# Turning the late tiles through device memory instead of on TensorE, in a hybrid encoder layer on one core

## The chip, the cores and the metric

One core of a Trainium2 chip runs the whole program. The metric is the time of one execution on the device in microseconds (us). The kernel before has a median of 942.22 us over 3 runs (942.02 to 943.11).

## The reference

One encoder layer over 256 tokens with 2048 channels, all in float32. The input is normalised and modulated by vectors made from `c` (`w_ada`), multiplied by one wide matrix `w_in`, and its columns feed three branches:

```
mod = silu(c) @ w_ada + b_ada;  shift, scale, gate = split(mod, 3)
h = rms_norm(x, norm_g) * (1 + scale) + shift
proj = h @ w_in      # pool_u, pool_z, q, k, v, attn_z, conv_a, conv_b, conv_z, gates
y_pool = multiscale_pool(pool_u, pool_w, pool_scale) * silu(pool_z)
y_attn = window_attention(q, k, v, attn_sink) * silu(attn_z)
y_conv = conformer_conv(conv_a, conv_b, ...) * silu(conv_z)     # ends in @ conv_pw (1024 x 1024)
g_pool, g_attn, g_conv = split(sigmoid(gates), 3)
merged = g_pool * (y_pool @ w_branch_pool) + g_attn * (y_attn @ w_branch_attn) + g_conv * (y_conv @ w_branch_conv)
x = x + gate * (merged @ w_out)
out = rms_norm(x, final_g)
```

`shift`, `scale` and `gate` are vectors of 2048, one value for each channel. All matrices together are more than 150 MB, and each is read once.

## The kernel before

**Pieces.** All large products are cut into 152 pieces, numbered m = 0 to 151. A piece is 512 rows (four tiles of 128) by 512 columns of a weight matrix, 1 MB. A chunk is the set of pieces that add up into one block of 256 tokens x 512 columns; it fills one of two accumulators in PSUM, `acc_even` or `acc_odd`, which the chunks take in turn. Each float32 operand is split into a high half (`wh`, `act_h`) and a low half (`wl`, `act_l`), and a product takes three matmuls (lines 1246, 1247, 1248). With four tiles and two halves of the tokens a piece is 24 matmuls of 512 columns.

**The weights' way.** SyncE issues the load of a piece into one of four `raw` buffers. ScalarE rounds it to `wh` (L466) once the piece four places earlier has been used, VectorE subtracts to get `wl` (L759), and then the `raw` buffer is free for the next load. In the loop over m ScalarE and VectorE both end step m with their share of piece m + 4. Every engine works its list in order, so a wait in step m holds back all that stands behind it.

**The order of the late pieces.** 88 to 91 `zc1`; 92 to 95 the attention branch `ba0`, `ba1`; 96 to 103 the gates `ga2`, `ga3`; 104 to 107 `ba2`, `ba3`; 108 to 111 `pw0`, `pw1` (the pointwise product of the convolution); 112 to 119 `gc0`, `gc1`; 120 to 123 `bc0`, `bc1`; 124 to 131 `gc2`, `gc3`; 132 to 135 `bc2`, `bc3`; 136 to 151 the four result chunks `o0` to `o3`, four pieces each (K tiles 0 to 3, 4 to 7, 8 to 11, 12 to 15).

**LayerNorm of the convolution**, steps 92 to 101: VectorE sums (L1151, L1160), TensorE adds over partitions after pieces 93 and 97 (L1459), VectorE scales (L1168), ScalarE applies SiLU (L700) and takes the high half (L706), VectorE the low half (L1172).

**Transposes.** `zs_conv` (the gated convolution output, two blocks) and `merged` (the merged branches, four blocks of 512 channels) are in token layout and are needed with channels on partitions. For each of these six late blocks TensorE runs eight 128x128 transposes (`transpose4`, L1291) into a side bank, `side_a` or `side_b`; ScalarE copies the high half out (L474), VectorE the low half (L775). A semaphore `y_ready` counts the blocks that are done: `bc0` waits for 5 and 6, piece i of `o0` for 7 + i.

**Gate vector.** `gate` is made from 16 loads of 1 MB of `w_ada`, put between the loads of the pieces (GATE_AFTER). For each, VectorE runs four multiply-adds into `gate_sums` (L1083 and L1089, `gate_piece`), in the step that splits the piece of that number. After four loads ScalarE takes the high half (L717), VectorE the low half (L1187), TensorE sums over partitions with a matrix of ones (L1560, L1561, 512 columns each), and VectorE adds the row to `gate_rows` (L1194). Quarter q + 1 starts only when quarter q's matmuls are done.

**The end.** `o0` to `o2` are multiplied by the gate and added to the residual by VectorE (`residual`, L1098 and L1102), which frees the accumulator; ScalarE squares and sums them (L613), VectorE scales them by `final_g` (L1110). For `o3` the gate is multiplied into the four weight pieces instead (`gate_weights`, L771): VectorE does that for piece m + 2 right behind the split of m, for m from 146 on, and ScalarE's split of pieces 148 to 151 waits for it. The last four pieces run by half of the tokens.

**GpSimd** only issues the small loads. Late in the kernel these are `x_res` (2 MB, L439), `final_rows` (L440) and `gate_rows` (L442).

Of the kernel before, what the change touches and what calls it, by code (L numbers as in the profile page):

```python
# [4 lines left out]
P = 128  # L5
D_MODEL, SEQ = 2048, 256
TH = SEQ // P
# [60 lines left out]
GATE_AFTER = (112, 113, 115, 116, 118, 119, 121, 122, 124, 125, 127, 128, 130, 131, 133, 134)  # L68
# [44 lines left out]
QUAD = 32  # L113


def program(nc, a, out):
# [71 lines left out]
    zs_conv = [at("zs_conv0", [P, TH, COLS], F32, 192 * KB), at("zs_conv1", [P, TH, COLS], F32, 196 * KB)]  # L188

# [40 lines left out]
    with ctx:  # L230
# [60 lines left out]
        merged_ready = sem("merged_ready")  # L291
        gate_summed, gate_rows_mm, gate_added = sem("gate_summed"), sem("gate_rows_mm"), sem("gate_added")
# [68 lines left out]
        def score_step(u):  # L361
            return 71 + 2 * u

# [40 lines left out]
        def _(pool):  # L404
# [10 lines left out]
            for row, name, rows in ((V_NORM_G, "norm_g", 16), (V_B_ADA, "b_ada", 32),  # L415
# [22 lines left out]
            pool.wait_ge(used, END["pw1"])  # L438
            pool.dma_start(x_res[:, :, :], x_rows).then_inc(x_res_loaded, 16)  # L439
            pool.dma_start(final_rows[:, :], a["final_g"].partition_broadcast(P)).then_inc(final_loaded, 16)  # L440
            pool.wait_ge(y_t, 4)
            pool.dma_start(gate_rows[:, :], a["b_ada"][0, 2 * D_MODEL:3 * D_MODEL].partition_broadcast(P)  # L442
                           ).then_inc(gate_b_loaded, 16)

        @block.scalar
        def _(act):
# [28 lines left out]

            def by_tiles(bank_):
                return bank_[:, :].rearrange("p (t s) -> p t s", t=4)
# [138 lines left out]
            for m in range(OPENING - WIDTH - RING + 1, M_END):  # L616
# [90 lines left out]
                if m in (111, 113):  # L707
                    b = (m - 111) // 2
                    spread(y_h[:, 4 * b:4 * b + 4, :], by_tiles((pa, pb)[b]), y_t, 3 + b, y_high)
                if m in (113, 119, 125, 131):  # L710
                    q = (m - 113) // 6
# [7 lines left out]
                if m in (131, 133, 135, 137):  # L719
                    j = (m - 131) // 2  # L720
                    spread(act_h[:, 4 * j:4 * j + 4, :], by_tiles((pb, pb, pa, pb)[j]), y_t, 5 + j, y_high)
                if m in (140, 144, 148):
                    for h in range(TH):
                        square_result((m - 140) // 4, h, (m - 140) // 4 + 1)
# [880 lines left out]
```

## Time and profile before

| | value |
|---|---|
| median of 3 runs | 942.22 us |
| the profiled execution, its own time | 942.33 us |
| its span | 940.5 us |
| TensorE matmul busy | 911.0 us (97%), 4211 matmuls |
| VectorE busy | 703.0 us (75%) |
| ScalarE busy | 420.6 us (45%) |
| GpSimd busy | 9.2 us (1%) |
| loads on the SyncE queue | 67.1% of the 16 DMA engines' span |
| read from memory | 217.24 MB |

The time has 1.8 us outside the span. The span is cut below by stretch. "PE" is TensorE's matmuls, "DVE" VectorE, "ACT" ScalarE, "POOL" GpSimd, and a trailing q means the queue of the engine. In a row of the timeline the first number is the start from the span's beginning, the second how long the row covers, and what stands in brackets is how long the engine was idle before it and which engine ended that. A matmul's 0.39 us is its own length; they overlap, so the step from one start to the next is what counts.

### The profile page before, as it was taken

The numbers are of one execution on the slowest core, as the hardware profiler recorded it, in microseconds if no ns is written. First come the engines' busy times: TensorE is split into PE (matmuls) and PEld (weight loads), VectorE is DVE, ScalarE is ACT, GpSimd is POOL, SyncE is SP. The second block draws the span as 40 slices with busy tenths as digits, with TensorE's granted clock in tenths as the row PEclk, the third lists the DMA queues.
The fourth block names the chain that finished last, engine by engine and source line by source line (L and its number), as shares of the span: only waits on it lengthen the run. The fifth ranks groups of instructions, "written<-read, shape, count | busy, mean of one in ns | idle before, by whom it ended". The sixth has DMA issues, their size and how long they took to land.

```text
span 940.5 us, 10296 instructions
## 1 busy us (share of the span) xinstructions
PE 911.0 (97%) x4211; PEld 732.9 (78%) x4211; DVE 703.0 (75%) x794; ACT 420.6 (45%) x388; POOL 9.2 (1%) x26
## 2 busy tenths in 40 slices
PE   1999999999999999999999999999999999999996
PEld 1667777888888888888877777888888888888885
DVE  4778787878968777767688786685687988865783
ACT  3445252645344334444375655347433443444332
POOL 2000000000000000000000000000000000000000
PEclk9999999999999999999999999999999999999999
DMA  9999999855446556555545456656879998955512
GB/s 337 387 386 386 385 332 388 311 179 179 160 155 213 189 182 208 193 179 179 183 138 171 139 159 149 208 171 153 271 241 394 374 335 276 352 207 191 182 45 90
DMA packets 108208, 220.01 MB, mean 234 GB/s; under 512 B 3858, under 2 KB 3938, under 8 KB 107393
## 3 DMA queue, kind: packets, MB, share of 16 engines
q1 hardware_dynamic: 106768, 213.15, 67.1%
q0 software_dynamic: 1104, 5.42, 1.5%
q8 instruction: 33, 0.54, 0.2%
q10 hardware_dynamic: 288, 0.79, 0.2%
q14 instruction: 15, 0.11, 0.0%
HBM read 217.24 MB, written 2.10 MB: 233 GB/s over the span
## 4 chain that ended last, share of the span: by engine, by line
PE 90%; DVE 4%; DMA 3%; ACT 2%; issue 1%; SPq 0%; DVEq 0%; ACTq 0%
PE acc_odd L1246 13%; PE acc_odd L1248 13%; PE acc_odd L1247 13%; PE acc_even L1246 12%; PE acc_even L1248 12%; PE acc_even L1247 12%; PE side_a L1246 2%; PE side_a L1248 2%; PE side_a L1247 2%; PE side_b L1306 2%; DMA raw<-in_w_ada 1%; DVE gate_sums L1089 1%; DMA x_tok<-in_x 1%; PE side_b L1246 1%; PE side_a L1291 1%
## 5 line engine op out<-in xcount | busy, mean ns | idle before, releaser
L759 DVE TENSOR_TENSOR wl<-raw,wh 128x2048 fp32r<-128x2048 f32 x147 | 336.0, 2290 | 147.8 <-ACT wh L466 147.5
L466 ACT ACTIVATE wh<-raw 128x2048 fp32r<-128x2048 f32 x147 | 280.2, 1913 | 261.3 <-PE acc_odd L1248 105.7
L1246 PE MATMUL acc_odd<-wh,act_h 128*128 128x512 f32 x432 | 169.8, 393 | 0.0
L1246 PE MATMUL acc_even<-wh,act_h 128*128 128x512 f32 x430 | 169.7, 395 | 0.0
L1247 PE MATMUL acc_odd<-wl,act_h 128*128 128x512 f32 x432 | 168.2, 389 | 0.0
L1248 PE MATMUL acc_odd<-wh,act_l 128*128 128x512 f32 x432 | 168.2, 389 | 0.0
L1248 PE MATMUL acc_even<-wh,act_l 128*128 128x512 f32 x430 | 167.6, 390 | 0.0
L1247 PE MATMUL acc_even<-wl,act_h 128*128 128x512 f32 x430 | 167.4, 389 | 0.0
L974 DVE SCALAR_TENSOR_TENSOR conv_slots<-conv_slots,taps 128x256 f32<-128x256 f32 x240 | 100.2, 479 | 0.2
L1246 PEld LDWEIGHTS acc_even<-wh,act_h 128*128 128x128 f32 x430 | 80.7, 188 | 19.5 <-issue 2.8
L1246 PEld LDWEIGHTS acc_odd<-wh,act_h 128*128 128x128 f32 x432 | 81.1, 188 | 18.9 <-issue 2.2
L1248 PEld LDWEIGHTS acc_odd<-wh,act_l 128*128 128x128 f32 x432 | 81.1, 188 | 17.1
L1248 PEld LDWEIGHTS acc_even<-wh,act_l 128*128 128x128 f32 x430 | 80.7, 188 | 17.1
L1247 PEld LDWEIGHTS acc_odd<-wl,act_h 128*128 128x128 f32 x432 | 81.1, 188 | 16.4
L1247 PEld LDWEIGHTS acc_even<-wl,act_h 128*128 128x128 f32 x430 | 80.8, 188 | 16.1
L805 DVE SCALAR_TENSOR_TENSOR ada_sums<-raw,small,ada_sums 128x512 f32<-128x512 f32 x60 | 45.1, 752 | 7.8 <-DMA raw<-in_w_ada 5.9
L1089 DVE SCALAR_TENSOR_TENSOR gate_sums<-raw,small,gate_sums 128x512 f32<-128x512 f32 x60 | 45.0, 751 | 1.7
L1246 PE MATMUL acc_odd<-wh,y_h 128*128 128x512 f32 x96 | 37.6, 392 | 0.0
L1246 PE MATMUL acc_even<-wh,y_h 128*128 128x512 f32 x96 | 37.5, 390 | 0.0
L1248 PE MATMUL acc_even<-wh,y_l 128*128 128x512 f32 x96 | 37.4, 389 | 0.0
L1248 PE MATMUL acc_odd<-wh,y_l 128*128 128x512 f32 x96 | 37.4, 389 | 0.0
L1247 PE MATMUL acc_odd<-wl,y_h 128*128 128x512 f32 x96 | 37.4, 389 | 0.0
(294 smaller groups left out, 925.8 us busy)
## 6 DMA issues: line engine op xcount, KB each, us to landing
raw<-in_w_in SPq DMA_DIRECT2D x106, 1024.0 KB, 5.1
raw<-in_w_ada SPq DMA_DIRECT2D x48, 1024.0 KB, 9.3
raw<-in_w_out SPq DMA_DIRECT2D x16, 1024.0 KB, 5.0
raw<-in_w_branch_pool SPq DMA_DIRECT2D x8, 1024.0 KB, 5.0
raw<-in_w_branch_attn SPq DMA_DIRECT2D x16, 512.0 KB, 6.7
raw<-in_w_branch_conv SPq DMA_DIRECT2D x8, 1024.0 KB, 6.4
raw<-in_conv_pw SPq DMA_DIRECT2D x4, 1024.0 KB, 5.9
x_tok<-in_x SPq DMA_DIRECT2D x2, 1024.0 KB, 9.2
```

Of the source, the lines that this page charges most:

```text
L466: nc.scalar.activation(wh[:, m % RING], raw[SLOT_OF[g]][:, :, :], ACT.Copy).then_inc(high_done, 1)
L759: nc.vector.tensor_tensor(wl[:, m % RING], raw[SLOT_OF[load_of(m)]][:, :, :], wh[:, m % RING].bitcast(F32), ALU.subtract).then_inc(raw_don ...
L805: last = nc.vector.scalar_tensor_tensor(ada_sums[:, :], src, column, ada_sums[:, :], ALU.mult, ALU.add)
L974: ins = nc.vector.scalar_tensor_tensor(sums, window, tap, sums, ALU.mult, ALU.add)
L1089: last = nc.vector.scalar_tensor_tensor(gate_sums[:, :], src, column, gate_sums[:, :], ALU.mult, ALU.add)
L1246: nc.tensor.matmul(sums, xh, wh[:, slot, i, :], start=begin, stop=False)
L1247: nc.tensor.matmul(sums, xh, wl[:, slot, i, :], start=False, stop=False)
L1248: return nc.tensor.matmul(sums, xl, wh[:, slot, i, :], start=False, stop=end)
L1291: ins = nc.tensor.transpose(dst[:, SEQ * t + P * h:SEQ * t + P * (h + 1)], src(h, t), ident[:, :])
L1306: ins = nc.tensor.matmul(pb[rows, 0:COLS], c_wide[:, PK * i + t, :], raw[SLOT_OF[g]][:, t, :], start=(i == 0), stop=(i == 3), tile_positio ...
```

## The change

The six late blocks are no longer transposed on TensorE. VectorE transposes 32x32 squares (two instructions of 128x512 a block, `turn_blocks`) into a buffer `blocks`; GpSimd stores that to a scratch array in device memory with four DMAs of 32 partitions each (`store_blocks`), waits until all have landed, and loads it back in the other layout (one DMA for each block of `zs_conv`, two for each of `merged`). ScalarE and VectorE then take the halves from SBUF instead of PSUM. The two `blocks` buffers alternate, and the last two blocks also wait until the block two before them is back.

The 16 gate loads start after piece 98 instead of 112; the steps of the gate's halves and sums move to 101, 110, 120, 130 (ScalarE and VectorE) and 102, 111, 121, 131 (TensorE). The four gate rows each get a half of a side bank of their own, and are added into `gate_rows` at 123, 124, 128 and 134.

`o0` and `o1` alternate: pieces 136 to 143 are `o0` 0, `o1` 0, `o0` 1, `o1` 1 and so on, so each K block of `merged` is first needed two pieces later than the last. `residual` for `o0` moves from step 140 to 143, and the first two `scale_result` from 142 and 146 to 145 and 146. GpSimd's `gate_rows`, `x_res` and `final_rows` loads come later.

```diff
+TURNING = ("o0", "o1")
+START = sum(_pieces for _, _pieces in CHUNKS) - 4 * PK
...
+        if _name in TURNING:
+            _at = START + 2 * _i + TURNING.index(_name)
...
-GATE_AFTER = (112, 113, 115, 116, 118, 119, 121, 122, 124, 125, 127, 128, 130, 131, 133, 134)
+GATE_AFTER = (98, 100, 102, 104, 107, 109, 111, 113, 116, 118, 121, 123, 126, 128, 131, 133)
...
+    blocks = [at(f"blocks{s}", [P, 4, 4, TH, QUAD], F32, (176 + 4 * s) * KB) for s in range(2)]
+    scratch = [nc.dram_tensor(f"turned_{g}", (QUAD, 4, 4 * TH, 4, QUAD), F32, kind="Internal").ap() for g in range(TURNS)]
...
+            def store_blocks(g):
+
+                pool.wait_ge(blocks_ready, g + 1)
+                for a_ in range(4):
+                    pool.dma_start(scratch[g].rearrange("j b n a i -> j (b n) a i")[:, :, a_, :],
+                                   blocks[g % 2][QUAD * a_:QUAD * (a_ + 1), :, :, :, :].rearrange("j b t h i -> j (b t h) i")
+                                   ).then_inc(blocks_stored, 16)
+                pool.wait_ge(blocks_stored, 16 * 4 * (g + 1))
+
+            def load_merged(g):
+                rows = scratch[g].rearrange("j b (q n) a i -> q b j (n a i)", q=2)
+                for q in range(2):
+                    pool.dma_start(by_channels(g)[:, q, :, :].rearrange("p t s -> p (t s)"), rows[q]
+                                   ).then_inc(turned[g], 16)
+
+            for b in range(2):
+                store_blocks(b)
+                pool.dma_start(zs_conv[b][:, :, :].rearrange("p h c -> p (h c)"),
+                               scratch[b].rearrange("j b n a i -> b j (n a i)")).then_inc(turned[b], 16)
+            pool.wait_ge(y_ready, 6)
...
+            for g in range(2, TURNS):
+                store_blocks(g)
+                load_merged(g)
...
-                if m in (113, 119, 125, 131):
-                    q = (m - 113) // 6
+                if m in (118, 119):
+                    b = m - 118
+                    spread(y_h[:, 4 * b:4 * b + 4, :], turned_tiles(b), turned[b], 16, y_high)
+                if m in (101, 110, 120, 130):
+                    q = (101, 110, 120, 130).index(m)
                     act.wait_ge(raw_done, raws(LOAD_OF["gate", q, 3]))
...
+                if m in (132, 133, 138, 140):
+                    j = (132, 133, 138, 140).index(m)
+                    act.wait_ge(used, END["gc3"])
+                    spread(high_tiles(j), turned_tiles(2 + j), turned[2 + j], 16 * 2, y_high)
...
+            def turn_blocks(g, src):
+
+                for h in range(TH):
+                    last = nc.vector.transpose(blocks[g % 2][:, :, :, h, :].rearrange("p b t i -> p t b i"),
+                                               src[:, h, :].rearrange("p (t b j) -> p t b j", t=4, b=4))
+                last.then_inc(blocks_ready, 1)
...
+                if m == 112:
+                    for b in range(2):
+                        dve.wait_ge(*freed(f"pw{b}"))
+                        turn_blocks(b, zs_conv[b][:, :, :])
...
+                if m in (122, 124, 134, 136):
+                    j = (122, 124, 134, 136).index(m)
+                    dve.wait_ge(merged_ready, 9 + j)
+                    if j > 1:
+                        dve.wait_ge(turned[j], 16 * 2)
+                    turn_blocks(2 + j, merged[:, :, bass.ts(j, COLS)])
+                if m in (101, 110, 120, 130):
+                    dve.wait_ge(sums_high, (101, 110, 120, 130).index(m) + 1)
                     nc.vector.tensor_tensor(gate_low[:, :], gate_sums[:, :], gate_high[:, :].bitcast(F32), ALU.subtract
                                             ).then_inc(sums_low, 1)
...
-                if m in (140, 144, 148):
-                    if m == 140:
+                if m in (132, 133, 138, 140):
+                    j = (132, 133, 138, 140).index(m)
+                    low_halves(7 + j, high_tiles(j), low_tiles(j), turned_tiles(2 + j))
+                if m in (143, 144, 148):
+                    if m == 143:
                         dve.wait_ge(gate_added, 4)
                         dve.wait_ge(x_res_loaded, 16)
-                    residual((m - 140) // 4)
-                if m in (142, 146, 150):
-                    scale_result((m - 142) // 4)
+                    residual((143, 144, 148).index(m))
+                if m in (145, 146, 150):
+                    scale_result((145, 146, 150).index(m))
...
-                elif name == "o0":
+                elif name in TURNING:
                     pe.wait_ge(y_ready, 7 + i)
...
-                if m in (131, 133, 135, 137):
-                    j = (m - 131) // 2
-                    pe.wait_ge(merged_ready, 9 + j)
-                    if j == 2:
-                        pe.wait_ge(gate_added, 4)
-                    else:
-                        pe.wait_ge(y_ready, (6, 7, 0, 8)[j])
-                    transpose4((pb, pb, pa, pb)[j], block_of(merged, COLS * j), y_t)
+                if m in (102, 111, 121, 131):
+                    q = (102, 111, 121, 131).index(m)
+                    pe.wait_ge(sums_low, q + 1)
+                    pe.wait_ge(var_ready, 2)
+                    pe.wait_ge(y_ready, 4)
+                    nc.tensor.matmul(gate_bank(q), ones_high[:, :], gate_high[:, :], start=True, stop=False)
+                    nc.tensor.matmul(gate_bank(q), ones_high[:, :], gate_low[:, :], start=False, stop=True
+                                     ).then_inc(gate_rows_mm, 1)
```

## Rows read from the trace of the kernel before

**Rows 1.** Windows: start:end, span, busy time and instructions of each engine, clock, DMA

```profile
600.00:640.00 40.00, 40.00 (x178) 33.09 (x177) 35.72 (x21) 17.05 (x10) 0.00 (x0) 1.00 0.59 171
700.00:770.00 70.00, 69.91 (x316) 57.57 (x315) 57.91 (x54) 28.66 (x20) 1.83 (x3) 1.00 1.01 369
840.00:870.00 30.00, 30.00 (x142) 24.96 (x142) 17.80 (x12) 12.90 (x9) 0.00 (x0) 1.00 0.59 201
```

**Rows 2.** Timeline of ScalarE, two splits in a row, one piece apart

```profile
883.38 1.92 ACT L466 ACTIVATE wh<-raw 128x2048 fp32r<-128x2048 f32 x1 [3.52 <-PE acc_odd L1248]
888.82 1.92 ACT L466 ACTIVATE wh<-raw 128x2048 fp32r<-128x2048 f32 x1 [3.52 <-PE acc_odd L1248]
```

**Rows 3.** Timeline of TensorE around a transpose of eight

```profile
706.13 0.39 PE L1248 MATMUL acc_odd<-wh,conv_low 128*128 128x512 f32 x1
706.37 1.03 PE L1291 MATMUL side_a<-ident,zs_conv 128*128 128x128 f32 x8
707.16 0.47 PE L1246 MATMUL acc_even<-wh,act_h 128*128 128x512 f32 x1
707.47 0.39 PE L1247 MATMUL acc_even<-wl,act_h 128*128 128x512 f32 x1
```

**Rows 4.** Timeline of TensorE before the first gate row

```profile
724.27 0.39 PE L1248 MATMUL acc_even<-wh,act_l 128*128 128x512 f32 x1
724.75 0.50 PE L1560 MATMUL side_a<-gate_high,ones_high 128*128 128x512 f32 x1
```

**Rows 5.** Timeline of VectorE, steps 94 to 98

```profile
616.64 2.29 DVE L759 TENSOR_TENSOR wl<-raw,wh 128x2048 fp32r<-128x2048 f32 x1
620.73 2.29 DVE L759 TENSOR_TENSOR wl<-raw,wh 128x2048 fp32r<-128x2048 f32 x1 [1.80 <-ACT wh L466]
...
625.34 3.84 DVE L1160 TENSOR_REDUCE ln_stat<-squares 128x256 f32<-128x2048 f32 x1
```

**Rows 6.** Timeline of VectorE, two gate pieces: quarter's first, and a later one

```profile
694.17 0.48 DVE L1083 TENSOR_SCALAR gate_sums<-raw,small 128x512 f32<-128x512 f32 x1
694.69 2.33 DVE L1089 SCALAR_TENSOR_TENSOR gate_sums<-raw,small,gate_sums 128x512 f32<-128x512 f32 x3
...
712.51 3.11 DVE L1089 SCALAR_TENSOR_TENSOR gate_sums<-raw,small,gate_sums 128x512 f32<-128x512 f32 x4
715.53 1.22 DVE L1180 TENSOR_TENSOR zs_conv<-acc_odd,zs_conv 128x1024 f32<-128x1024 f32 x1
```

**Rows 7.** Timeline of VectorE, steps 99 to 102

```profile
654.13 2.29 DVE L759 TENSOR_TENSOR wl<-raw,wh 128x2048 fp32r<-128x2048 f32 x1 [1.32 <-ACT wh L466]
656.34 2.28 DVE L1172 TENSOR_TENSOR conv_low<-conv_slots,c_h 128x2048 fp32r<-128x2048 f32 x1
```

**Rows 8.** Timeline of ScalarE: pieces 97 and 102 end, halves of the gate

```profile
629.66 1.92 ACT L466 ACTIVATE wh<-raw 128x2048 fp32r<-128x2048 f32 x1 [3.52 <-PE acc_even L1248]
...
657.34 1.92 ACT L466 ACTIVATE wh<-raw 128x2048 fp32r<-128x2048 f32 x1 [1.43 <-PE acc_odd L1248]
...
754.67 0.63 ACT L717 ACTIVATE gate_high<-gate_sums 128x512 fp32r<-128x512 f32 x1 [0.83 <-DVE gate_sums L1089]
```

**Rows 9.** Timeline of VectorE: low half of the gate, and the tail

```profile
724.00 0.69 DVE L1187 TENSOR_TENSOR gate_low<-gate_sums,gate_high 128x512 fp32r<-128x512 f32 x1 [0.90 <-ACT gate_high L717]
...
892.98 2.28 DVE L771 TENSOR_TENSOR raw<-raw,gate_rows 128x2048 f32<-128x2048 f32 x1
895.18 1.22 DVE L1098 TENSOR_TENSOR out_tmp<-acc_odd,gate_rows 128x1024 f32<-128x1024 f32 x1
...
911.02 4.49 DVE L759 TENSOR_TENSOR wl<-raw,wh 128x2048 fp32r<-128x2048 f32 x2
```

**Rows 10.** DMA issues: queue, number, KB, us from issue to landing

```profile
x_res<-in_x POOLq DMA_DIRECT2D x1, 2048.0 KB, 10.8
pool_w<-in_pool_w POOLq DMA_DIRECT2D x1, 1024.0 KB, 6.2
...
gate_rows<-in_b_ada POOLq DMA_DIRECT2D x1, 1024.0 KB, 7.8
...
small<-in_attn_sink POOLq DMA_DIRECT2D x1, 8.0 KB, 2.7
```

**Rows 11.** Groups of GpSimd: busy, mean ns of one issue, idle before

```profile
L433 POOL DMA_DIRECT2D pool_w<-in_pool_w x1 | 0.9, 937 | 0.0
...
L442 POOL DMA_DIRECT2D gate_rows<-in_b_ada x1 | 0.5, 541 | 11.4 <-PE side_b L1291 11.4
```

More of the change, by code:

```diff
@@ L113 @@
 QUAD = 32
+TURNS = 6
 def program(nc, a, out):
@@ L291, in program @@
         merged_ready = sem("merged_ready")
+        blocks_ready, blocks_stored = sem("blocks_ready"), sem("blocks_stored")
+        turned = [sem(f"turned_{g}") for g in range(TURNS)]
         gate_summed, gate_rows_mm, gate_added = sem("gate_summed"), sem("gate_rows_mm"), sem("gate_added")
@@ L362, in score_step, with by_tiles, gate_bank, turned_tiles @@
             return 71 + 2 * u
+        def by_tiles(bank_):
+            return bank_[:, :].rearrange("p (t s) -> p t s", t=4)
+        def gate_bank(q):
+            return (pa, pb)[q // 2][:, bass.ts(q % 2, COLS)]
+        def turned_tiles(g):
+            return by_channels(g) if g >= 2 else zs_conv[g][:, :, :].rearrange("p h (t s) -> p (h t) s", t=2)
+        def high_tiles(j):
+            return act_h[:, 4 * j:4 * j + 4, :].rearrange("p (q t) s -> p q t s", q=2)
+        def low_tiles(j):
+            return act_l[:, 4 * j:4 * j + 4, :].rearrange("p (q t) s -> p q t s", q=2)
+        def by_channels(g):
+            return merged[:, :, bass.ts(g - 2, COLS)].rearrange("p q (t s) -> p q t s", t=2)
         @block.sync
@@ L474, in spread @@
                 nc.scalar.activation(dst, src, ACT.Copy).then_inc(signal, 1)
-            def by_tiles(bank_):
-                return bank_[:, :].rearrange("p (t s) -> p t s", t=4)
             act.wait_ge(c_loaded, 16)
@@ L1193, in _ @@
                     row = gate_rows[:, bass.ts(q, COLS)]
-                    nc.vector.tensor_tensor(row, row, pa[:, 0:COLS], ALU.add).then_inc(gate_added, 1)
-                if m in (131, 133, 135, 137):
-                    j = (m - 131) // 2
-                    tiles = slice(4 * j, 4 * j + 4)
-                    low_halves(7 + j, act_h[:, tiles, :], act_l[:, tiles, :], (pb, pb, pa, pb)[j])
-                if m in (140, 144, 148):
-                    if m == 140:
+                    nc.vector.tensor_tensor(row, row, gate_bank(q), ALU.add).then_inc(gate_added, 1)
+                if m in (132, 133, 138, 140):
+                    j = (132, 133, 138, 140).index(m)
+                    low_halves(7 + j, high_tiles(j), low_tiles(j), turned_tiles(2 + j))
+                if m in (143, 144, 148):
+                    if m == 143:
                         dve.wait_ge(gate_added, 4)
                         dve.wait_ge(x_res_loaded, 16)
-                    residual((m - 140) // 4)
-                if m in (142, 146, 150):
-                    scale_result((m - 142) // 4)
+                    residual((143, 144, 148).index(m))
+                if m in (145, 146, 150):
+                    scale_result((145, 146, 150).index(m))
                 for i in range(taps_done, taps_done + TAPS_AT.get(m, 0)):
```

46 lines of the change are left out of this document (10 added, 36 removed).

## The prediction

> **What bounds the kernel now.** I read the page first: TensorE is busy for 97% of the span and nearly all of the chain that ended last is its matmuls. Then the windows of the stretch that the change touches [rows 1]: TensorE is busy for 40.00 of 40, 69.91 of 70 and 30.00 of 30 us, at full granted clock. It is the only engine without slack, and a saving counts only if it shortens TensorE's own list or a wait in it. The beat is in ScalarE's splits [rows 2]: each starts when a piece ends, and they are 5.44 us apart, so a piece is 24 matmuls at 0.227 us. VectorE is the second engine: 35.72 of 40 us busy in steps 93 to 98 and 57.91 of 70 behind piece 111, but only 17.80 of 30 in the stretch 840 to 870. The DMA engines are full in the stretch of the gate loads (1.01) and 0.59 busy in the other two. No TensorE wait comes from that, so moving the gate loads gives back nothing by itself.
>
> **Removed: six transposes.** Around one of them [rows 3] the start of the last matmul before and of the second after are 1.34 us apart; without the eight transposes these two steps are 0.46 us. So 0.88 us each, 6 x 0.88 = 5.3 us less. The three other edits to TensorE's list are neutral in work: four pairs of gate matmuls stay, and pieces 136 to 143 only change order. Before the first gate row TensorE waits: 724.27 to 724.75 is 0.48 instead of 0.23 us [rows 4]; the third row's is alike. These two waits, 0.5 us, go with the old places. Credit: 5.8 us.
>
> **Wait 1, at piece 97 (0.6 us).** Gate piece 0 now follows the split of piece 98 on VectorE. It costs 2.85 us (694.17 to 697.02) [rows 6]. VectorE was idle for 1.80 us there, until 620.73 [rows 5]; free at 618.85, it now starts that split at 621.7, 1.0 us late. The reduction that started at 625.34 and took 3.84 us ends at 630.15 instead of 629.18. TensorE's column sums stand behind piece 97, which ended at 629.57 [rows 8]: they wait 0.6 us.
>
> **Wait 2, at piece 102 (5.3 us): the dearest step.** TensorE sums the first gate row right behind piece 102, and for that waits for the low half of the sums. The last gate piece of this quarter is bound to the split of piece 104, which VectorE started at 654.13 [rows 7], held there by ScalarE's long LayerNorm step. Behind it stand now: the gate piece, 3.03 us [rows 6], the low half of the convolution, which was next at 656.34 (2.2 us) [rows 7], and the low half of the gate, 0.69 us [rows 9]; ScalarE's high half (0.63) [rows 8] fits beside the second. 656.34 + 3.03 + 2.2 + 0.69 = 662.3. Piece 102 ended at 657.26 (ScalarE's split behind it started at 657.34) [rows 8]. That is 5.0 us; the split of 104 itself slips by about 0.8 (gate pieces 0 and 1 push the scaling before SiLU by 3.7 us, of which some 3 had been slack), while piece 102 slips by the 0.6 of wait 1. I take 5.3. Behind the waiting sum stand pieces 103 and on, so TensorE gets nothing back. The second, third and fourth rows (pieces 111, 121, 131) have their last gate piece one piece earlier against the wait; by the same count they just fit, within 0.5 us.
>
> **Wait 3, at the end of `o0` (2.4 us), and 0.2 us before `o1`.** Before, `o0` ended four pieces ahead of `o2`, which needs the same accumulator. Now it ends with piece 142 and `o2` starts at 144, one piece (5.44 us) later. VectorE comes to `residual` only behind the split of 146 and the gating of 148: ScalarE 1.92 [rows 2], VectorE 2.2 and 2.2, then the multiply that frees the bank, 1.22 [rows 9], and some 0.25 of hand-overs: 7.8 us. TensorE waits 2.4. The same sum without the gating is 5.6 us for `bc3`'s bank before the first piece of `o1`: 0.2 us.
>
> **Wait 4, in the last four pieces (1.0 us).** The late `residual` pushes ScalarE's square and sum, the splits of 147 to 149, and the two `scale_result` that now stand before the splits of 149 and 150. Before, the pair of splits that ends the list ran 911.02 to 915.5 [rows 9]; the first of the pair was 2.4 us ahead of its need. Adding the steps up, the split of 150 ends some 6.1 us later, TensorE's need only 2.7 us later (the sum so far): 6.1 - 2.7 - 2.4 = 1.0 us.
>
> So without anything from the DMAs: -5.8 + 0.6 + 5.3 + 0.2 + 2.4 + 1.0 = +3.7 us. VectorE's twelve transposes lie in its slack; the nearest rows for one of 128x512 are 0.48 and 0.69 us [rows 6, 9], I take 0.62, or 1.24 us a block.
>
> **Wait 5, the way through memory.** The trace has no such store. The last two blocks decide, since `merged` block 2 is done two pieces ahead of block 3, and GpSimd's list is serial: store, wait, load, next store. Take the end of piece 135 as 0. Block 2 is ready at -2.4, block 3 at +8.0 (split of 139, merge, turn). TensorE needs block 3 at piece 142, 6 x 5.44 + 0.2 = 32.8; with the halves (ScalarE 1.0, VectorE 1.2) and hand-overs it must be back at 30.4. With S for a store and L for a load: back at -2.4 + S + 1.0 + S + L, if S is over 9.4. L: two issues of 0.5 us, then 4.5 us (rows from 2.7 us for 8 KB to 7.8 for 1 MB [rows 10]), 5.5 in all. S: four issues of 1024 runs of 128 bytes each. Floor for one: its issue, 0.94 us, as `pool_w` of 1024 runs [rows 11]. Ceiling: `pool_w` itself, eight times the bytes in as many runs, 6.2 less the 2.7 of a tiny one [rows 10], 3.5 us. I take 2.0, between, because count speaks for one end and bytes for the other. Four are 8 us alone; beside the weight loads, which hold 0.59 of the DMA engines [rows 1], about 11.5, plus 2.7 to land: S = 14.3. Back at 32.7, 2.3 us late; I take 2.5 us. At the floor (S about 7) nothing waits. At the ceiling S is 16.7 alone and over 20 beside the loads: 7 to 15 us here, and some more at `bc0` and the third gate row.
>
> The Trainium skill ("DMA: Bandwidth & Descriptors", Specifications) puts the least transfer for full rate at 512 bytes and says smaller ones make the DMA engine read, modify and write. It speaks against runs of 128 bytes, towards the ceiling; no row here shows such a store to memory.
>
> **Sum.** 3.7 + 2.5 = +6.2 us on the profiled execution's 942.33 (span 940.5 and 1.8 around it), 948.5 us. That execution is 0.1 us over the median, which I don't correct for.
>
> **Rivals.**
> 1. The memory way is hidden: S under 13. For it: 128 KB a DMA is little, and nothing else is on GpSimd's queue. 942.3 + 3.7 = 946.0. Chance 0.30.
> 2. The memory way binds outright, S 17 or more: tile 3 is late by 7 to 15 us, and blocks 0 and 1 are late for `bc0` too, since both are turned in one step at 112 and pass GpSimd one behind the other; each 2 us of S adds 4 at the end. 953 to 970, most likely 958. For it: 24,576 short runs in all. Chance 0.22.
> 3. GpSimd can't write its DMA work while VectorE runs: every issue waits for the end of a split or gate piece (2.3 to 3 us [rows 6]), 4 x 2.3 = 9 us a store, 2 x 9 - 4 late at the end: about 960. Against it: `gate_rows` was issued at 0.54 us [rows 11] in the middle of a split, and landed in 7.8 us [rows 10] with the DMAs full. The Trainium skill ("SBUF — State Buffer", SBUF: two separate sides) has this as a lock of the port that VectorE and GpSimd share. By the issue row the trace doesn't bear it out. Chance 0.04.
> 4. The other sign: wait 2 is not there. The one mechanism is the place of VectorE's last gate piece: if ScalarE handed over piece 104 at least 5 us sooner, or the row's matmuls found their input before piece 102 ends at 657.9, wait 2 is 0, and with S under 13 the sum is 3.7 - 5.3 = -1.6, 940.7 us. It decides faster from 3.5 us of the 5.3 on. Against it: rows 7 are the present order, and nothing in the change makes ScalarE's LayerNorm step earlier. Chance 0.04 for faster; 0.06 for within 0.2%, where it is only part gone.
>
> My forecast, 947 to 953 by wait 5 of 1 to 7 us, has 0.34. Slower by over 0.2% (1.9 us, about what a measurement of this kernel can tell from no change) is then 0.34 + 0.30 + 0.22 + 0.04 = 0.90. Range 944.8 to 963: rival 1 at the low end with 1 us of error in the waits, most of rivals 2 and 3 at the top; about 0.10 lies below and 0.10 above.
>
> **What would show it.** In the profile after: no L1291 rows on `merged` or `zs_conv`; the first gate row's matmul with an idle of 4.5 to 6 us before it, ended by VectorE's low half; an idle of 2 to 3 us before the first matmul of piece 144, ended by L1098's successor in the file; the fourth block's wait before piece 142, ended by the low half, itself behind a DMA. Wrong would be: a first gate row without a wait (rival 4), waits at pieces 120 or 121 (rival 2), or GpSimd issue rows of over 2 us (rival 3).

## The result, and the profile of the changed kernel

The changed kernel has a median of 953.96 us over 4 runs (953.34 to 956.9), the kernel before 942.25 us (942.02 to 943.11) in the same comparison. The ratio is 1.013, 95% interval 1.0118 to 1.0142: 12 us slower, where +6 was predicted. The sign was right. The time lies inside the stated range, but above my forecast of 947 to 953 and in the part that belongs to rival 2, and rival 2's cause was not at work: that it came to lie there is no merit of the sum.

The profiled execution of the changed kernel took 956.9 us, with a span of 955.1, 14.6 over the span before. That is 3 us more than its median and the longest of the four, so the sizes below are those of a slightly long execution.

TensorE's timeline, stretches around its longest idle times. Columns: start, duration, engine, line, operation, operands, count, and in brackets the idle time before it with what ended it.

```profile
657.43 0.39 PE L1312 MATMUL acc_odd<-wl,act_h 128*128 128x512 f32 x1
657.66 0.39 PE L1313 MATMUL acc_odd<-wh,act_l 128*128 128x512 f32 x1
663.12 0.80 PE L1615 MATMUL side_a<-gate_high,ones_high 128*128 128x512 f32 x1 [5.07 <-DVE gate_low L1253]
663.72 0.63 PE L1616 MATMUL side_a<-gate_low,ones_high 128*128 128x512 f32 x1
664.15 0.63 PE L1311 MATMUL acc_odd<-wh,act_h 128*128 128x512 f32 x1
664.57 0.63 PE L1312 MATMUL acc_odd<-wl,act_h 128*128 128x512 f32 x1
...
826.54 0.39 PE L1313 MATMUL acc_odd<-wh,act_l 128*128 128x512 f32 x1
830.93 0.80 PE L1615 MATMUL side_b<-gate_high,ones_high 128*128 128x512 f32 x1 [4.00 <-DVE gate_low L1253]
...
899.49 0.39 PE L1313 MATMUL acc_odd<-wh,act_l 128*128 128x512 f32 x1
902.16 0.50 PE L1311 MATMUL acc_even<-wh,act_h 128*128 128x512 f32 x1 [2.29 <-DVE out_tmp L1154]
...
929.27 0.39 PE L1313 MATMUL acc_odd<-wh,act_l 128*128 128x512 f32 x1
930.51 0.50 PE L1311 MATMUL acc_odd<-wh,act_h 128*128 128x512 f32 x1 [0.85 <-DVE wl L809]
```

To read a loss out of it, take the distance between two starts and subtract the usual step, 0.227 us: 663.12 - 657.66 - 0.23 = 5.2 us. A second loss has no bracket at all: behind the first gate row the matmuls start 0.42 apart instead of 0.227 (664.15 and 664.57) and last 0.63 instead of 0.39. The windows show why (columns as in [rows 1], the last three being the granted clock, the DMA share and GB/s):

```profile
663.00:669.00 6.00, 5.88 (x14) 4.63 (x15) 4.47 (x3) 1.74 (x1) 0.00 (x0) 0.50 1.05 316
669.00:680.00 11.00, 11.00 (x50) 9.12 (x49) 3.60 (x4) 6.04 (x4) 0.00 (x0) 1.00 0.45 155
...
831.00:836.50 5.50, 5.50 (x13) 4.36 (x14) 4.10 (x2) 4.61 (x4) 0.00 (x0) 0.51 0.74 255
836.50:845.00 8.50, 8.50 (x39) 7.02 (x38) 4.92 (x4) 2.86 (x2) 0.00 (x0) 1.00 0.60 226
```

TensorE ran at 1.2 GHz for 6 us behind the 5.2 us wait, and again behind the 4.2 us wait. Between 663 and 669 it is 5.88 us busy, so this loss can't be found by looking for idle time. Its size also differs from run to run. The 5.2 us wait at piece 102 stands unchanged in four of the kernels below, and the loss behind it was 1.9, 2.2, 1.6 and 1.9 us there (`e3_xres_late`, `e4_long`, `e8_res142`, `e10_by_b`) as against 2.8 here. In `e10_by_b` the granted clock was 0.50 already from 660.5 us on, with TensorE idle, and full again from 666.7; here it was still 0.90 from 660.5 to 662.7, and the low stretch fell on the matmuls.

All that TensorE lost or gained, each by the distance of starts:

| Place | us |
|---|---|
| six transposes, old gate-row waits gone | -5.8 |
| piece 97, column sums (wait 1) | +0.6 |
| first gate row, piece 102 (wait 2) | +5.2 |
| low clock behind it | +2.8 |
| third gate row, piece 121 | +1.1 |
| fourth gate row, piece 131 | +4.2 |
| low clock behind it | +2.6 |
| first piece of `o1`, first of `o2` (wait 3) | +0.25, +2.4 |
| last four pieces (wait 4) | +1.0 |
| sum; difference of the spans | +14.4; +14.6 |

The fourth gate row wasn't in my sum. Its chain in the trace, on ScalarE and then on VectorE:

```profile
816.02 1.92 ACT L517 ACTIVATE wh<-raw 128x2048 fp32r<-128x2048 f32 x1 [4.89 <-DMA raw<-in_w_branch_conv]
822.22 1.92 ACT L517 ACTIVATE wh<-raw 128x2048 fp32r<-128x2048 f32 x1 [4.28 <-DMA raw<-in_w_branch_conv]
829.52 0.63 ACT L765 ACTIVATE gate_high<-gate_sums 128x512 fp32r<-128x512 f32 x1 [5.39 <-DVE gate_sums L1145]
```

```profile
824.17 2.29 DVE L809 TENSOR_TENSOR wl<-raw,wh 128x2048 fp32r<-128x2048 f32 x1 [3.90 <-ACT wh L517]
826.38 3.11 DVE L1145 SCALAR_TENSOR_TENSOR gate_sums<-raw,small,gate_sums 128x512 f32<-128x512 f32 x4
830.18 0.69 DVE L1253 TENSOR_TENSOR gate_low<-gate_sums,gate_high 128x512 fp32r<-128x512 f32 x1 [0.70 <-ACT gate_high L765]
```

The last gate piece is bound to VectorE's split, the split to ScalarE's, and ScalarE's to a weight load that lands 4.28 us after ScalarE is free. The matmuls of the weights have pieces in hand and don't notice. The gate row has none, so it takes the whole delay. The releaser in TensorE's bracket, `gate_low`, is only the last link. The DMA issues (columns as in [rows 10]) and ScalarE's waits for loads (us in total, times, longest) belong to it:

```profile
raw<-in_w_branch_conv SPq DMA_DIRECT2D x8, 1024.0 KB, 12.4
turned<-blocks POOLq DMA_DIRECT2D x24, 128.0 KB, 5.8
...
merged<-turned POOLq DMA_DIRECT2D x8, 256.0 KB, 8.3
...
zs_conv<-turned POOLq DMA_DIRECT2D x2, 512.0 KB, 14.4
```

```profile
ACT wh L517 <- DMA raw<-in_w_branch_conv: 22.7, 5, 6.6
ACT wh L517 <- DMA raw<-in_w_in: 22.3, 7, 6.8
```

The landing times are medians, and the waits are those from 600 to 955 us. In the kernel before, the eight loads of `in_w_branch_conv` landed in 6.4 us, and in the same stretch ScalarE waited 7.2 and 3.4 us for these two. GpSimd's timeline of the last two blocks shows how long the way through memory took:

```profile
853.68 3.10 POOL L472 DMA_DIRECT2D turned<-blocks  x4 [42.52 <-DVE blocks L830]
862.31 1.38 POOL L480 DMA_DIRECT2D merged<-turned  x2 [5.53 <-DMA turned<-blocks]
864.70 3.10 POOL L472 DMA_DIRECT2D turned<-blocks  x4 [1.00 <-DVE blocks L830]
876.34 1.38 POOL L480 DMA_DIRECT2D merged<-turned  x2 [8.54 <-DMA turned<-blocks]
```

A store of four is 862.31 - 853.68 = 8.6 us and 11.6 us here, not 14.3, and TensorE doesn't wait for block 3. The stores of the first four blocks took 6.4, 17.3, 11.5 and 12.4 us, also without a TensorE wait of their own.

### The profile page after: what moved, and what is told of

It reads as the page before. It is cut to its first block, busy times and chain, and to the rows that moved or that the text cites. A ratio compares the mean times of both kernels' runs of the same rounds, so it can differ in the third digit from the quotient of the medians.

```text
span 955.1 us, 10249 instructions
## 1 busy us (share of the span) xinstructions
PE 912.0 (95%) x4163; PEld 731.6 (77%) x4163; DVE 710.1 (74%) x806; ACT 420.2 (44%) x388; POOL 34.8 (4%) x60
## 2 busy tenths in 40 slices
DMA packets 112593, 226.32 MB, mean 237 GB/s; under 512 B 6706, under 2 KB 6786, under 8 KB 111777
## 3 DMA queue, kind: packets, MB, share of 16 engines
q0 software_dynamic: 5488, 11.73, 4.4%
## 4 chain that ended last, share of the span: by engine, by line
PE 77%; DVE 9%; DMA 6%; ACT 4%; issue 3%; SPq 0%; DVEq 0%; ACTq 0%
PE acc_even L1311 11%; PE acc_even L1313 11%; PE acc_even L1312 11%; PE acc_odd L1311 10%; PE acc_odd L1312 10%; PE acc_odd L1313 10%; DMA raw<-in_w_branch_conv 3%; DVE wl L809 2%; PE side_a L1311 2%; PE side_a L1313 2%; PE side_a L1312 2%; ACT wh L517 2%; PE side_b L1371 2%; DVE gate_sums L1145 1%; DMA raw<-in_w_ada 1%
## 5 line engine op out<-in xcount | busy, mean ns | idle before, releaser
L1313 PEld LDWEIGHTS acc_odd<-wh,act_l 128*128 128x128 f32 x432 | 81.7, 189 | 17.3
L472 POOL DMA_DIRECT2D turned<-blocks x24 | 18.7, 811 | 611.7 <-DVE blocks L830 611.7
L1312 PE MATMUL acc_even<-wl,y_h 128*128 128x512 f32 x96 | 38.2, 398 | 0.0
## 6 DMA issues: line engine op xcount, KB each, us to landing
raw<-in_w_branch_conv SPq DMA_DIRECT2D x8, 1024.0 KB, 12.4
```

Of the source, the lines that this page charges most:

```text
L472: pool.dma_start(scratch[g].rearrange("j b n a i -> j (b n) a i")[:, :, a_, :], blocks[g % 2][QUAD * a_:QUAD * (a_ + 1), :, :, :, :].rearr ...
L1312: nc.tensor.matmul(sums, xh, wl[:, slot, i, :], start=False, stop=False)
L1313: return nc.tensor.matmul(sums, xl, wh[:, slot, i, :], start=False, stop=end)
```

## The experiments

Ten kernels ran, each compared with the kernel before on its own chip (medians there 942.0 to 942.3 us). The ratio is to the kernel before.

| Kernel | median us (lowest to highest) | ratio, 95% interval |
|---|---|---|
| `e1_row1_104` | 947.24 (945.62 to 948.2) | 1.0052, 1.0037 to 1.0067 |
| `e2_filler` | 953.40 (951.2 to 955.12) | 1.0118, 1.0099 to 1.0137 |
| `e3_xres_late` | 951.36 (948.19 to 954.26) | 1.0097, 1.007 to 1.0124 |
| `e4_long` | 951.09 (949.53 to 951.62) | 1.0096, 1.008 to 1.0113 |
| `e5_all` | 937.31 (936.5 to 938.75) | 0.9948, 0.9933 to 0.9962 |
| `e6_gates_late` | 960.20 (959.47 to 962.05) | 1.0195, 1.0178 to 1.0212 |
| `e7_alt_only` | 947.63 (947.32 to 948.06) | 1.0056, 1.0041 to 1.0071 |
| `e8_res142` | 948.56 (945.79 to 950.9) | 1.0064, 1.0043 to 1.0086 |
| `e9_all_by_b` | 936.75 (936.56 to 937.49) | 0.9943, 0.993 to 0.9955 |
| `e10_by_b` | 947.59 (947.41 to 948.76) | 1.006, 1.0044 to 1.0075 |

**The first gate row two pieces later.**

```diff
-                if m in (102, 111, 121, 131):
-                    q = (102, 111, 121, 131).index(m)
+                if m in (104, 111, 121, 131):
+                    q = (104, 111, 121, 131).index(m)
```

> The changed kernel with one edit: TensorE sums the first gate row behind piece 104 instead of 102. My theory: in the changed kernel the wait there is 5.2 us (5.46 less the usual 0.23) and the matmuls behind it run at half the clock for 5.7 us, which costs another 2.6 us; the input is ready 5.4 us after the end of piece 102, so behind 104 nothing waits. The time falls by 7 to 8 us, from 954 to 946 or 947. Rival, the clock is not caused by the wait: it falls by 5.2 only. Rival, what is saved here is lost behind it because VectorE or the loads set the pace in the stretch 740 to 840: it falls by under 3 us.

947.24 us, 6.7 less than the changed kernel. In its profile TensorE is busy for 60.00 of the 60 us from 640 to 700 at full clock, and the gate row's matmul starts 0.23 us behind the one before it, without an idle time. Wait 2 and the low clock behind it are worth 8.0 us and both are gone; 2.2 us come back as new waits of 1.65 and 0.57 us before the pieces of `bc0`. At the third and at the fourth row the wait was 1.4 us each, without a low clock.

**The wait filled with matmuls.**

```diff
+                    for _ in range(22 if q == 0 else 0):
+                        nc.tensor.matmul(gate_bank(q), act_h[:, 0, 0:P], act_h[:, 0:2, :], start=True, stop=True)
                     pe.wait_ge(sums_low, q + 1)
```

> The changed kernel with 22 matmuls of 512 columns on data that is not used, put on TensorE ahead of its wait for the first gate row (5.0 us of work in a wait of 5.2 us; they write the bank that the row's sum then starts anew). The wait is not shortened. If the low clock behind the wait comes from TensorE's idling, these 2.6 us go and the time falls to about 951.4. If it comes from something else in that stretch (its other engines), the time stays at 954 or rises with what the filler is too long.

The timeline of TensorE at the same place in this kernel:

```profile
657.53 0.39 PE L1313 MATMUL acc_odd<-wh,act_l 128*128 128x512 f32 x1
657.75 5.15 PE L1615 MATMUL side_a<-act_h 128*128 128x512 f32 x22
662.99 0.50 PE L1617 MATMUL side_a<-gate_high,ones_high 128*128 128x512 f32 x1
663.32 0.39 PE L1618 MATMUL side_a<-gate_low,ones_high 128*128 128x512 f32 x1
663.55 0.39 PE L1311 MATMUL acc_odd<-wh,act_h 128*128 128x512 f32 x1
```

The gate row comes as late as before, 662.99, but the matmul behind it starts 0.23 us later, not 0.42. The granted clock was 1.00 from 640 to 670. So the low clock follows from TensorE's idleness in the wait and not from the gate row or what else runs in that stretch. The time as a whole is nearly that of the changed kernel, 953.40 where 951.4 was expected. In the profiled execution the third row waits 2.1 us, not 1.1, a piece behind it 0.8, and the fourth row 3.9 with 1.7 of low clock. I read this as follows, which these rows fit but don't show by themselves: what is saved ahead of waits that end with a load is waited for at the load. The four runs lie 4 us apart, so the medians decide nothing here; the rows do.

**`x_res` loaded after the last block.** The load moves from ahead of the blocks of `merged` to behind them on GpSimd's queue.

> The changed kernel with the 2 MB load of x_res moved behind the last block on GpSimd's list. Question: why does TensorE wait 4.2 us for the fourth gate row behind piece 131, which I had put at under 0.5 us. Theory A: the weight loads are late because x_res (5 us of all DMA engines, issued at 765.6) runs beside them: the wait at 131, with its 2.6 us of low clock, and the 1.1 us at 121 shrink, together 4 to 7 us less, 947 to 950. Theory B: the stores of short runs (issued at 784 to 800) hold the DMA engines: the time falls by under 2 us.

Its four runs lie 6 us apart (948.19 to 954.26), so 951.36 beside 953.96 decides little. The profiled execution is the fastest of them. In it the third row waits 0.4 us and the fourth not at all. What speaks beyond the spread is ScalarE's wait for the loads of `in_w_in`. It is 21.8 to 27.1 us in all five profiles with `x_res` and the gate loads at the places of the changed kernel and the loads back uncut (the changed kernel, `e1_row1_104`, `e2_filler`, `e4_long`, `e8_res142`), none here, and 5.4 us in `e5_all`, where `x_res` is late too. So this load does take part in the delay, but I can't say for how many microseconds of the whole.

**Stores in long runs.** The scratch is written in another order, 4 KB a run instead of 128 bytes, and read back as before; so what returns is not the tiles in their places.

```diff
-                    pool.dma_start(scratch[g].rearrange("j b n a i -> j (b n) a i")[:, :, a_, :],
-                                   blocks[g % 2][QUAD * a_:QUAD * (a_ + 1), :, :, :, :].rearrange("j b t h i -> j (b t h) i")
+                    pool.dma_start(scratch[g].rearrange("(x j) b n a i -> x (j b) (n a i)", x=4)[a_, :, :],
+                                   blocks[g % 2][QUAD * a_:QUAD * (a_ + 1), :, :, :, :].rearrange("j b t h i -> j (b t h i)")
```

> The changed kernel, but each of the 24 stores writes runs of 4 KB (32 partitions x 1024 values, contiguous in the scratch array) instead of 128 bytes; as many bytes and DMAs. The scratch then holds the values in another order, so the output is not the reference's. Theory B of the run before (short runs hold the DMA engines): a store of four lands in 5 to 7 us instead of 11 to 17, the DMA share in 780 to 820 falls well below 1, the wait at piece 131 (4.2 us and 2.6 us of low clock) goes: 945 to 949. Theory A (x_res and the gate loads fill the engines): the stores land sooner, but the waits stay and the time falls by under 2 us.

951.09 us. The DMA issues of this kernel:

```profile
turned<-blocks POOLq DMA_DIRECT2D x24, 128.0 KB, 5.0
...
merged<-turned POOLq DMA_DIRECT2D x8, 256.0 KB, 8.6
...
zs_conv<-turned POOLq DMA_DIRECT2D x2, 512.0 KB, 13.2
```

By the median a DMA lands in 5.0 us instead of 5.8, and four issues take 2.0 us instead of 3.1. The median hides the larger part. A whole store, from GpSimd's first issue to its next instruction behind the wait, took 5.4, 15.4, 8.0, 9.9, 4.5 and 6.4 us for the six blocks, as against 6.4, 17.3, 11.5, 12.4, 8.6 and 11.6 in the changed kernel. In all eight other kernels with this way through memory the last two stores took 8.6 to 9.3 and 8.9 to 11.0 us, so there the short runs cost 2.5 to 5.2 us a store. The 15.4 us of block 1 have another cause, as `e10_by_b` will show. In its profiled execution, the fastest of the four, the third and fourth rows wait 0.4 us each, and ScalarE still waits 27.1 and 15.7 us for the two kinds of weight loads. So short runs are dear for the store itself and do little for the weight loads: the time is between what the two theories expected.

**The gate loads late, as in the kernel before.** `GATE_AFTER` and the four gate rows move to pieces 112 to 134.

```diff
-GATE_AFTER = (98, 100, 102, 104, 107, 109, 111, 113, 116, 118, 121, 123, 126, 128, 131, 133)
+GATE_AFTER = (112, 113, 115, 116, 118, 119, 121, 122, 124, 125, 127, 128, 130, 131, 133, 134)
...
-                if m in (102, 111, 121, 131):
+                if m in (114, 120, 126, 132):
```

> The changed kernel with the gate part undone: the loads after the pieces of the kernel before (112 to 134), the halves at steps 113, 119, 125, 131 and the rows' matmuls behind pieces 114, 120, 126, 132; the adding of the rows, the way through memory and the alternation stay. Theory 1, the early gate loads cost their two waits and low clock (0.6 + 5.2 + 2.4) and their late loads: 943 to 947. Theory 2, they are needed: with the loads of before (DMA share 1.0 from 700 to 770 already) and the stores on top, the weights come late, waits of several us appear between 112 and 135, and it is at 950 or above.

960.20 us, 6.2 over the changed kernel. Wait 2 is gone, though the first gate row still waits 1.6 us at its new place. ScalarE now waits 30.5 us for `in_w_branch_conv` and 14.2 for `in_w_in`, and TensorE 5.4 us at `bc0` and 5.05 before a gate row, both with the low clock behind them (1.9 and 1.7 us lost). This goes against the remark in the prediction that moving the gate loads gives back nothing by itself: with the traffic of the turned tiles beside them, the late places cost more than the early ones.

**The alternation alone.** The kernel before, its transposes and its gate loads as they were, with only the new order of pieces 136 to 143 and what belongs to it on VectorE.

> The kernel before with only the alternation of o0 and o1 and the moved steps of residual, squares and scaling (143, 144, 148; 145, 146, 150); transposes stay on TensorE. By my sum the waits of 0.2, 2.4 and 1.0 us that the changed kernel shows at the end (0.25, 2.44 and 1.01) belong to this part alone: 942.0 + 3.7 = 945.7 us. Rival, in the changed kernel they come from the late blocks and go without these: 942 to 943.

947.63 us, +5.3. The profile has 1.05 us before `o1`, 2.44 before `o2` and 1.0 in the last four pieces, 4.5 in all. Its span is 5.5 longer; of the rest, 0.55 us lies ahead of the edit and 0.45 is not accounted for. I had expected 945.7. The waits before `o2` and in the last pieces are the ones of my sum, so they belong to the alternation and not to the late blocks; the wait before `o1` is 1.05 us here and 0.25 in the changed kernel.

**`residual(0)` one step earlier.**

```diff
-                if m in (143, 144, 148):
-                    if m == 143:
+                if m in (142, 144, 148):
+                    if m == 142:
...
-                    residual((143, 144, 148).index(m))
+                    residual((142, 144, 148).index(m))
```

> The changed kernel with one edit: residual for o0 at step 142, ahead of VectorE's split of 146 and gating of 148. My theory of the 2.44 us at the end of o0: the bank is freed 4.4 us sooner, the wait goes, and with it the 1.0 us in the last pieces: 954.0 - 3.4 = 950.5 us. Rival, the moved work only makes the splits late: a wait as long in front of pieces 145 to 147, 953 to 955.

948.56 us (945.79 to 950.9). The waits of 2.4 and 1.0 us are no longer in the profile; VectorE's multiply starts at 892.29, after 1.24 us of idle time ended by TensorE: it now waits for the accumulator. In the changed kernel it was the accumulator's next user that waited for VectorE's list. The drop of 5.4 us is more than these 3.4; part of it is the spread at the load-bound waits.

**Places chosen so that nothing waits.** Gate rows behind pieces 104, 111, 122 and 133, `x_res` after the last block, and `residual(0)` at 142, in the changed kernel.

> The changed kernel with the four places mended that the profile names: TensorE sums the gate rows behind pieces 104, 111, 122 and 133 instead of 102, 111, 121 and 131; x_res is loaded behind the last block; residual for o0 stands at step 142, ahead of the split of 146 and the gating of 148, instead of 143. My theory: from 947.2 (row 1 behind 104 alone) another 2.7 us of waits at the third and fourth row and 3.4 us at the end of o0 and in the last pieces go: 940 to 942, about the time of before, because two waits at the first pieces of bc0 (2.2 us: blocks 0 and 1 back late) eat half of the 5.8 us that the transposes gave. Rival, the loads set the pace from 740 to 820 whatever TensorE waits for: what goes at the rows comes back as waits at pieces 120 to 131, and it stays above 943.

937.31 us: faster than both kernels. Left are 0.6 us at piece 97, 1.43 before the first piece of `bc0` and 0.24 before `o1`; no low clock. By the terms, -5.8 + 0.6 + 1.4 + 0.2 = -3.6, and the span is 936.9, 3.6 less than before.

**Loads back cut by partitions.** In the changed kernel, each load back becomes four DMAs of 32 partitions; everything else stays.

```diff
-                rows = scratch[g].rearrange("j b (q n) a i -> q b j (n a i)", q=2)
-                for q in range(2):
-                    pool.dma_start(by_channels(g)[:, q, :, :].rearrange("p t s -> p (t s)"), rows[q]
+                for b in range(4):
+                    part = slice(QUAD * b, QUAD * (b + 1))
+                    pool.dma_start(by_channels(g)[part, :, :, :].rearrange("p q t s -> p q (t s)"),
+                                   scratch[g].rearrange("j b (q n) a i -> b j q (n a i)", q=2)[b]
```

> The changed kernel with only the loads back cut into four DMAs of 32 partitions. If the confinement to 4 engines makes them slow, the loads of blocks 0 and 1 land in 5 to 8 us instead of 14.4, but TensorE waits little for these blocks in the changed kernel, so the time falls by under 2 us: 952 to 954. If they only move load from one place to another, the same.

947.59 us, 6.4 less than the changed kernel, which I had not expected. Its DMA issues, and ScalarE's waits for loads in the stretch 600 to 955:

```profile
raw<-in_w_branch_conv SPq DMA_DIRECT2D x8, 1024.0 KB, 9.4
...
merged<-turned POOLq DMA_DIRECT2D x16, 128.0 KB, 5.6
zs_conv<-turned POOLq DMA_DIRECT2D x8, 128.0 KB, 5.9
```

```profile
ACT wh L519 <- DMA raw<-in_w_branch_conv: 3.6, 1, 3.6
```

The bytes are the same and the DMA share is as high (1.02 from 780 to 820), yet the weight loads land in 9.4 us instead of 12.4 and ScalarE's waits for them fall from 45 us to 3.6. TensorE waits at neither the third nor the fourth row; wait 2 and waits 3 and 4 are as they were, with 1.9 us of low clock behind wait 2. GpSimd's store of block 1, which runs beside the load back of block 0, takes 740.02 - 730.13 = 9.9 us instead of 17.3.

The load back of block 1 itself, 0.52 MB, can be seen in the DMA queues: packets, MB and share of the 16 engines, for SyncE's queue (q1, the weights) and GpSimd's (q0). First the changed kernel from 749 to 760.6 us, then this one from 744 to 748.2:

```profile
q1 hardware_dynamic: 949, 1.88, 68.0%
q0 software_dynamic: 512, 0.51, 21.9%
...
q1 hardware_dynamic: 294, 0.57, 56.8%
q0 software_dynamic: 186, 0.50, 47.8%
```

Uncut, the load moved for 11.6 us on 0.219 x 16 = 3.5 engines in the mean; cut, the same bytes moved in 4.2 us on 7.6 engines, beside the weights on 9.1.

The same form in the combined kernel:

> The kernel with the four places mended (937.3 us), and the loads back from the scratch array cut otherwise: four DMAs of 32 partitions for each block instead of one (blocks 0 and 1) or two of 128 partitions whose outermost dimension in memory has size 4. In the run before, these loads of 512 KB took 12 to 18 us to land, as against 7.8 us for the 1 MB of gate_rows from the same queue, and TensorE waited 1.4 us for block 0 at piece 120. Theory, by the Trainium skill's rule on how many DMA engines a transfer uses (DMA: Bandwidth & Descriptors, Why a DMA increments its semaphore by 16 and not by 1): an outermost size of 4 confines the load to 4 engines; cut into parts of 32 it uses all 16, lands in 5 to 8 us, and the 1.4 us go: 936. Rival: the loads are slow because the weight loads fill the engines at 725 to 760 (DMA share 0.95): they land as late as before and the time stays at 937 or rises with the two or three more issues of 0.5 us.

936.75 us. The 1.43 us before `bc0` are gone too, and 0.25 before `o1` are all that is left behind piece 97. By the terms, -5.8 + 0.6 + 0.25 = -4.95; the span is 935.7, 4.8 less than before. Its median is 0.56 us under that of `e5_all`, which is within the spread of the runs of either, so the removed wait is seen in the profile only. Of the two it is the version to keep.

## Why the prediction was right in sign and too small

The four waits that were counted came out one by one, and they give the sign. The size, +12 for +6, is made up otherwise than predicted: wait 5 was not there, and a low clock and two later rows that had no term were.

**Credit, 5.8 us: borne out.** `e9_all_by_b` removes nearly every new wait and lands 4.8 us below the span before.

**Wait 1, 0.6: measured 0.6.** VectorE's reduction started at 626.31 where I had counted 1.0 us behind 625.34.

**Wait 2, 5.3: measured 5.2.** The four steps on VectorE stand in the trace in the order of the sum: 654.95 the split, 657.15 gate piece, 660.18 `conv_low`, 662.39 `gate_low`, ended at 663.1. Two pieces later the wait was gone (`e1_row1_104`).

**Missing from the sum: the low clock.** I counted each wait at its length and the matmuls behind it at 0.227 us. After waits of 5.2 and 4.2 us they ran at 1.2 GHz for some 6 us each, 2.8 and 2.6 us lost. That it hangs on the idleness, `e2_filler` shows. In the other kernels the same wait 2 cost 1.6 to 2.2 us of this, so about 1 us of the 5.4 is the luck of this execution.

**The failed step: "the second, third and fourth rows ... just fit, within 0.5 us".** I carried over from wait 2 the count of VectorE's steps and assumed that the weight splits come on time. The second row fitted (no wait behind piece 111), the third cost 1.1 and the fourth 4.2, plus its clock: 7.9 us for a term set at nothing. Its split waited for a load. The prediction said "No TensorE wait comes from that" of the full DMA engines, which held for the kernel before, whose load-bound waits of ScalarE had slack behind them. I then costed the new transfers only by when their own data are back, never by what they do to the loads that run beside them. The wait at the third row stands behind piece 121, one of the places where I had said that waits would speak for rival 2; it came from late weights and not from a late block. Rival 2 had the memory way as a bound, but through its own lateness (S of 17 and more); the stores were as slow as that once, at 17.3 us, without a wait at TensorE for it.

What makes the weight loads late is shown in part. Three edits each relieve them. By the medians, the loads back cut by partitions give 6.4 us (`e10_by_b`), long runs 2.9 (`e4_long`), `x_res` moved 2.6 (`e3_xres_late`, uncertain). Only the first also ends ScalarE's waits: 3.6 us for weight loads, against 45 in the changed kernel, 42.8 in `e4_long` and 20.5 in `e3_xres_late`. So the form of the loads back is the largest share, and no single load has all of it.

The form decides on how many engines a load back moves, 3.5 and 7.6 in the mean by the rows of `e10_by_b`. The Trainium skill ("DMA: Bandwidth & Descriptors", Why a DMA increments its semaphore by 16 and not by 1) says that the number of DMA engines is the largest up to 16 that divides the slowest dimension of both access patterns, the source's and the destination's. The patterns in the scratch array have a 4 there, 32 when cut, so by that rule it is 4 engines and then 16. The trace agrees with the first (3.5 in the mean, under 4) and doesn't contradict the second (7.6, over 4, beside the weights). The landing times fit too, 14.4 us for 512 KB against 5.9 us for each quarter of it. The cut also lowers the packets of GpSimd's queue from 5488 to 3408. The fall is all in packets under 512 bytes (6706 to 4625 on the pages), and the bytes moved are the same (226.3 MB); what these small packets cost by themselves no run shows. How a load that holds few engines makes the weight loads beside it late is not shown packet by packet either.

**Wait 3, 2.4 and 0.2, and wait 4, 1.0: measured 2.4, 0.25 and 1.0.** `e8_res142` shows the cause as named, VectorE's order, and that one step earlier frees it.

**Wait 5, 2.5: measured 0.** S was 8.6 and 11.6 us for the last two blocks, under the 13 of rival 1. ScalarE took block 3 at 884.02, as soon as it had landed. That is 28.2 us behind the end of piece 135 (855.8), where the prediction had it back at 32.7 and needed at 30.4; VectorE's half ended at 886.35, and piece 142 started at 888.84. The over-sized term was the store, 14.3 us. The load back was under-sized, 5.5 against 7.7 us for block 3 and 10.9 for block 2. The Trainium skill's 512 bytes as the least transfer for full rate ("DMA: Bandwidth & Descriptors", Specifications) point the right way. By the trace, these two stores took 4.5 and 6.4 us in runs of 4 KB (`e4_long`).

**Rival 3:** the 24 issues of stores took 0.77 to 0.87 us each (3.1 for four), the four of the last block, 3.10 us from 864.70 on, beside VectorE's split from 863.97 to 866.22.

**Rival 4** can't reach what it was given a chance for. Without wait 2 its sum is -1.6 us, and "faster" was set at more than 1.9; the sum changes sign from 3.7 us of the wait on, not from 3.5. Wait 2 stood at its full size, so nothing hung on it.

So the terms for the changed kernel are 3.7 by the waits counted, 5.4 by the clock, 5.3 by the two later rows, 0 by wait 5: 14.4 against 14.6 by the spans.

**Still open.** How the 2.9 us of `e4_long` divide between the length of the runs and chance, and the 2.6 us between `e3_xres_late` and the changed kernel between `x_res` and chance; the runs of all versions with load-bound waits lie 2 to 6 us apart, those without within 2.3. Why ScalarE's late loads hurt `e6_gates_late` more than the changed kernel is argued from the crowding, not shown by an experiment of its own. Why the low clock behind one and the same wait costs 1.6 us in one kernel and 2.8 in another is open too.

## What to carry to other kernels

A wait of some microseconds on TensorE has a second part that no idle row shows: look at the step between matmuls and the granted clock in the window behind it. Something that a fully fed engine needs only once, such as a bias row, should be consumed some pieces after it can be made, not right after; moving it adds no work, and here two pieces gave 6.7 us. When new transfers go where the DMA engines are already full, cost them by what they do to the transfers beside them, and look at their access pattern first: the same bytes in another cut gave 6.4 us.

## What the runs showed of the hardware that I had not expected

- After idle times of 5.07 and 4.00 us the granted clock was 0.50 and 0.51 for about 6 us; after the 2.29 us before `o2` it stayed full in this kernel, but in `e4_long` and `e6_gates_late` the same 2.29 us were followed by 1.6 us of loss at the low clock (0.55 for 3.5 and 3.8 us). After 1.4 us at the fourth row of `e1_row1_104` there was none.
- A VectorE transpose of 128x512 by 32x32 blocks took 0.69 us, as a plain operation of that size does ([rows 9]).
- Four stores of 128 KB in runs of 128 bytes, from the first issue to the last landing, took 6.4 to 17.3 us in the changed kernel. Both form and company count: the last block's took 6.4 us instead of 11.6 in runs of 4 KB, and block 1's 9.9 instead of 17.3 when the load back beside it was cut.
- A load back of 512 KB whose slowest dimension in memory is 4 moved on 3.5 of the 16 DMA engines in the mean for 11.6 us; as four DMAs with a 32 there it moved on 7.6 for 4.2 us.
